# The first microseconds of a one-core transformer kernel: tokens in four transfers, squares shared out, narrowest bands scaled first

## The reference, cut to what matters

```python
def rms_norm(x, g):
    xf = x.astype(jnp.float32)
    y = xf * lax.rsqrt(jnp.mean(xf * xf, axis=-1, keepdims=True) + RMS_EPS)
    return (y * g.astype(jnp.float32)).astype(x.dtype)

def pool_mixer(h, w, scale):
    ...
    for g, win in enumerate(POOL_WINDOWS):      # (2, 4, 8, 16), 256 features each
        c = cs[:, :, g]                          # running sum over tokens
        lag = jnp.pad(c[:, :-win], ((0, 0), (win, 0), (0, 0)))
        mean = (c - lag) / jnp.minimum(n_avail, float(win))[:, None]
        outs.append(mean - hf[:, :, g])
    ...
    y = jnp.einsum('bsgc,gcd->bsgd', p, w).reshape(B, S, D)
    return y * scale
```

## Time and profile before

| what | value |
|---|---|
| median of 3 runs | 1299.62 us (1297.34, 1299.62, 1299.71) |
| the profiled execution, its own time | 1299.65 us |
| its span in the profile | 1297.9 us |
| PE busy (matmul) | 98% of the span |
| DVE busy | 71% |
| ACT busy | 47% |
| first matmul starts at | 6.14 us |

### The profile page before, as it was taken

One profiled execution on the slowest core, in us unless ns is written; L12 is line 12 of the kernel. 1 busy time (PEld: TensorE's weight loads), 2 busy tenths in 40 slices (PEclk: granted clock), 3 DMA queues, 4 the chain that ended last, 5 costly groups with the idle time before them and its releaser, 6 DMA issues.

```text
span 1297.9 us, 19342 instructions
## 1 busy us (share of the span) xinstructions
PE 1270.6 (98%) x7379; PEld 1109.1 (85%) x7379; DVE 916.4 (71%) x1217; ACT 605.3 (47%) x881; POOL 29.3 (2%) x29
## 2 busy tenths in 40 slices
PE   7999999999999999999999999999999999999997
PEld 7779999988888777788999998888888888888876
DVE  6897787874447766579788787454768388887554
ACT  6445454553334655444454455434323255666434
POOL 0510000000000000000000000000000000000000
PEclk9999999999999999999999999999999999999999
DMA  5322424332332111231332423223624221113311
GB/s 194 109 87 66 129 67 127 90 113 89 107 103 79 30 64 66 65 97 54 109 108 86 129 87 115 90 89 106 183 65 163 66 64 34 50 49 130 98 65 66
DMA packets 156963, 119.70 MB, mean 92 GB/s; under 512 B 15132, under 2 KB 153832, under 8 KB 156648
## 3 DMA queue, kind: packets, MB, share of 16 engines
q1 hardware_dynamic: 156848, 118.89, 29.9%
q10 hardware_dynamic: 56, 0.01, 0.0%
HBM read 114.70 MB, written 4.19 MB: 92 GB/s over the span
## 4 chain that ended last, share of the span: by engine, by line
PE 75%; DVE 13%; issue 4%; ACT 4%; DMA 2%; SPq 1%; DVEq 0%; ACTq 0%
PE psum L2338 22%; PE psum L2340 22%; PE psum L2339 22%; DMA w_raw<-in_ffn_w_up 2%; PE psum L2563 1%; PE psum L2586 1%; DVE w_lo L1596 1%; DVE w_lo L1409 1%; ACT w_hi L908 1%; PE psum L2748 1%; PE psum L2720 1%; ACT w_hi L802 1%; PE psum L2732 1%; DVE second_sum L1583 1%; DVE ffn_f L1551 1%
## 5 line engine op out<-in xcount | busy, mean ns | idle before, releaser
L2338 PE MATMUL psum<-terms_hi,w_hi 128*128 128x256 f32 x952 | 270.9, 285 | 3.0 <-DVE work L1607 2.6
L2339 PE MATMUL psum<-terms_lo,w_hi 128*128 128x256 f32 x952 | 270.1, 284 | 0.0
L2340 PE MATMUL psum<-terms_hi,w_lo 128*128 128x256 f32 x952 | 270.1, 284 | 0.0
L2338 PE MATMUL psum<-xg_hi,w_hi 128*128 128x512 f32 x544 | 220.8, 406 | 3.5 <-DVE squares L1536 1.9
L2340 PE MATMUL psum<-xg_hi,w_lo 128*128 128x512 f32 x544 | 212.3, 390 | 0.0
L2339 PE MATMUL psum<-xg_lo,w_hi 128*128 128x512 f32 x544 | 212.1, 390 | 0.0
L2338 PEld LDWEIGHTS psum<-terms_hi,w_hi 128*128 128x128 f32 x952 | 183.4, 193 | 4.5 <-DVE w_lo L1596 2.8
L2339 PEld LDWEIGHTS psum<-terms_lo,w_hi 128*128 128x128 f32 x952 | 183.4, 193 | 0.1
L2340 PEld LDWEIGHTS psum<-terms_hi,w_lo 128*128 128x128 f32 x952 | 183.4, 193 | 0.0
L2338 PE MATMUL psum<-act_hi,w_hi 128*128 128x512 f32 x352 | 137.2, 390 | 0.0
L2340 PE MATMUL psum<-act_hi,w_lo 128*128 128x512 f32 x352 | 136.9, 389 | 0.0
(11 more groups left out here) (404 smaller groups left out, 2201.2 us busy)
## 6 DMA issues: line engine op xcount, KB each, us to landing
w_raw<-in_ffn_w_gate SPq DMA_DIRECT2D x68, 256.0 KB, 3.4
w_raw<-in_ffn_w_up SPq DMA_DIRECT2D x68, 256.0 KB, 3.9
w_raw<-in_w_in SPq DMA_DIRECT2D x16, 1024.0 KB, 5.4
w_raw<-in_ffn_w_down SPq DMA_DIRECT2D x16, 768.0 KB, 4.5
w_raw<-in_ffn_w_down SPq DMA_DIRECT2D x16, 640.0 KB, 4.3
w_raw<-in_ffn_w_gate SPq DMA_DIRECT2D x5, 1024.0 KB, 5.1
w_raw<-in_ffn_w_up SPq DMA_DIRECT2D x5, 1024.0 KB, 5.2
w_raw<-in_mla_w_o SPq DMA_DIRECT2D x4, 1024.0 KB, 5.0
```

What stands on the lines that cost most here:

```text
L2338: pe.matmul(o, wh, xh, start=start, stop=False, skip_group_check=True)
L2339: pe.matmul(o, wh, xl, start=False, stop=False, skip_group_check=True)
L2340: return pe.matmul(o, wl, xh, start=False, stop=stop, skip_group_check=True)
```

## The change

Tokens come in four transfers of one block each, with a semaphore for each, and PE turns the seven chunks block by block. ACT squares blocks 0 and 2 and the first 512 features of block 3, DVE squares block 1 and the last 512 features of block 3, and DVE adds the two sums of block 3. Blocks 0 to 2 get their root and reciprocal ahead of block 3. The bands of the smallest width (144 columns, all that `pooled(0)` and `pooled(1)` use) are scaled ahead of the other three widths (432 columns). Two semaphores are folded into others (`ones_set` into `eps_set`, `mask_loaded` into `pos_loaded`).

```diff
-            for n in range(2):
-                sp.dma_start(x_tok[:, 2 * n:2 * n + 2, :], a["x"][0].rearrange("(i p) f -> p i f", p=P)[:, 2 * n:2 * n + 2]).then_inc(sem(f"x_loaded{n}"), 16)
-                if n == 0:
+            for i in range(NB):
+                sp.dma_start(x_tok[:, i, :], a["x"][0, i * P:(i + 1) * P, :]).then_inc(sem(f"x_loaded{i}"), 16)
+                if i == 0:
                     sp.dma_start(ident[:, :], a["c_ident"]).then_inc(sem("ident_loaded"), 16)
...
# ACT
-            act.wait_ge(sem("tok_squares"), NB)
-            act.activation(tok_stat[:, 1, :], tok_stat[:, 0, :], ACT.Sqrt, ...).then_inc(*mark("tok_root"))
+            act.wait_ge(sem("tok_squares"), 3)
+            act.activation(tok_stat[:, 1, 0:3], tok_stat[:, 0, 0:3], ACT.Sqrt, ...).then_inc(*mark("tok_root_early"))
+            act.wait_ge(sem("x_loaded3"), 16)
+            act.activation(h_tok[:, 3, 0:T], x_tok[:, 3, 0:T], ACT.Square, accum_out=tok_stat[:, 0, 3:4]).then_inc(*mark("tok_half"))
+            act.wait_ge(*at("tok_sum"))
+            act.activation(tok_stat[:, 1, 3:4], tok_stat[:, 0, 3:4], ACT.Sqrt, ...).then_inc(*mark("tok_root"))
+            act.wait_ge(*at("tok_rstd_early"))
+            act.wait_ge(sem("band_loaded"), 16)
+            odd_band(1, slice(0, 1))
             act.wait_ge(*at("tok_rstd"))
-            act.wait_ge(sem("band_loaded"), 16)
-            for i in (1, 3):
-                act.activation(band_tok[:, i, :, :], band[:, :, 0, :], ACT.Copy, scale=tok_stat[:, 2, i:i + 1])...
+            odd_band(3, slice(0, 1))
+            odd_band(1, slice(1, 4))
+            odd_band(3, slice(1, 4))
...
# PE
-            for n in range(2):
-                pe.wait_ge(sem(f"x_loaded{n}"), 16)
+            for i in range(NB):
+                pe.wait_ge(sem(f"x_loaded{i}"), 16)
                 for m in range(7):
-                    mm = turn_x(m, (2 * n, 2 * n + 1))
-                    if n:
+                    mm = turn_x(m, (i,))
+                    if i + 1 == NB:
                         mm.then_inc(sem("x_turned"), 1)
...
-                    pe.wait_ge(sem("band_odd" if i % 2 else "band_even"), i // 2 + 1)
+                    pe.wait_ge(sem("band_odd" if i % 2 else "band_even"), (0 if c < 2 else 2) + i // 2 + 1)
```

More of the change, by code:

```diff
@@ L746, in _ @@
         def _(pool):
-            pool.memset(ones[:, :], 1.0).then_inc(sem("ones_set"), 1)
+            pool.memset(ones[:, :], 1.0).then_inc(sem("eps_set"), 1)
             pool.memset(eps_col[:, 0:1], EPS).then_inc(sem("eps_set"), 1)
@@ L751, in _ @@
             pool.memset(eps_col[:, 3:4], 1.0).then_inc(sem("eps_set"), 1)
-            pool.wait_ge(sem("eps_set"), 4)
+            pool.wait_ge(sem("eps_set"), 5)
             pool.memset(eps_col[64:128, 3:4], -1.0).then_inc(sem("eps_set"), 1)
-            pool.wait_ge(sem("eps_set"), 5)
+            pool.wait_ge(sem("eps_set"), 6)
             MAGIC, TWO_PI = 1.5 * 2.0 ** 23, 6.283185307179586
@@ L758, in _ @@
             ang = sem("angle_step")
-            pool.wait_ge(sem("pos_loaded"), 32)
+            pool.wait_ge(sem("pos_loaded"), 48)
             pool.wait_ge(*at("mix_summed"))
@@ L814, in _, with odd_band @@
             for i in (0, 2):
-                act.wait_ge(sem(f"x_loaded{i // 2}"), 16)
+                act.wait_ge(sem(f"x_loaded{i}"), 16)
                 act.activation(h_tok[:, i, :], x_tok[:, i, :], ACT.Square, accum_out=tok_stat[:, 0, i:i + 1]).then_inc(sem("tok_squares"), 1)
-            act.wait_ge(sem("eps_set"), 5)
-            act.wait_ge(sem("tok_squares"), NB)
-            act.activation(tok_stat[:, 1, :], tok_stat[:, 0, :], ACT.Sqrt, scale=1.0 / D, bias=eps_col[:, 0:1]).then_inc(*mark("tok_root"))
+            act.wait_ge(sem("eps_set"), 6)
+            act.wait_ge(sem("tok_squares"), 3)
+            act.activation(tok_stat[:, 1, 0:3], tok_stat[:, 0, 0:3], ACT.Sqrt, scale=1.0 / D, bias=eps_col[:, 0:1]).then_inc(*mark("tok_root_early"))
+            act.wait_ge(sem("x_loaded3"), 16)
+            act.activation(h_tok[:, 3, 0:T], x_tok[:, 3, 0:T], ACT.Square, accum_out=tok_stat[:, 0, 3:4]).then_inc(*mark("tok_half"))
+            act.wait_ge(*at("tok_sum"))
+            act.activation(tok_stat[:, 1, 3:4], tok_stat[:, 0, 3:4], ACT.Sqrt, scale=1.0 / D, bias=eps_col[:, 0:1]).then_inc(*mark("tok_root"))
+            def odd_band(i, windows):
+                act.activation(band_tok[:, i, windows, :], band[:, windows, 0, :], ACT.Copy, scale=tok_stat[:, 2, i:i + 1]).then_inc(sem("band_odd"), 1)
+            act.wait_ge(*at("tok_rstd_early"))
+            act.wait_ge(sem("band_loaded"), 16)
+            odd_band(1, slice(0, 1))
             act.wait_ge(*at("tok_rstd"))
-            act.wait_ge(sem("band_loaded"), 16)
-            for i in (1, 3):
-                act.activation(band_tok[:, i, :, :], band[:, :, 0, :], ACT.Copy, scale=tok_stat[:, 2, i:i + 1]).then_inc(sem("band_odd"), 1)
+            odd_band(3, slice(0, 1))
+            odd_band(1, slice(1, 4))
+            odd_band(3, slice(1, 4))
             def late_copy(m):
@@ L1420, in chain @@
                 dve.tensor_tensor(sq_sum[:, :], sq_sum[:, :], squares[:, m % 2, :], ALU.add).then_inc(dv, 1)
[L1422 to L1425, removed]
+            dve.wait_ge(sem("x_loaded1"), 16)
+            dve.scalar_tensor_tensor(h_tok[:, 1, :], x_tok[:, 1, :], 1.0, x_tok[:, 1, :], ALU.mult, ALU.mult, accum_out=tok_stat[:, 0, 1:2])\
+               .then_inc(sem("tok_squares"), 1)
+            dve.wait_ge(sem("x_loaded3"), 16)
+            dve.scalar_tensor_tensor(h_tok[:, 3, T:2 * T], x_tok[:, 3, T:2 * T], 1.0, x_tok[:, 3, T:2 * T], ALU.mult, ALU.mult, accum_out=tok_stat[:, 0, 4:5])\
+               .then_inc(*mark("tok_low"))
+            dve.wait_ge(*at("tok_low"))
+            dve.wait_ge(*at("tok_half"))
+            dve.tensor_tensor(tok_stat[:, 0, 3:4], tok_stat[:, 0, 3:4], tok_stat[:, 0, 4:5], ALU.add).then_inc(*mark("tok_sum"))
+            dve.wait_ge(*at("tok_root_early"))
+            dve.reciprocal(tok_stat[:, 2, 0:3], tok_stat[:, 1, 0:3]).then_inc(*mark("tok_rstd_early"))
             def early_copy(m):
@@ L1429, in early_copy, with even_band @@
                 dve.tensor_copy(xT[:, m, :], bank[m][:, :]).then_inc(sem("xT_early"), 1)
+            def even_band(i, windows):
+                dve.tensor_scalar(band_tok[:, i, windows, :], band[:, windows, int(i == 0), :], tok_stat[:, 2, i:i + 1], None, ALU.mult).then_inc(sem("band_even"), 1)
             early_copy(0)
+            dve.wait_ge(*at("tok_rstd_early"))
+            dve.wait_ge(sem("band_loaded"), 16)
+            even_band(0, slice(0, 1))
+            even_band(2, slice(0, 1))
             dve.wait_ge(*at("tok_root"))
-            dve.reciprocal(tok_stat[:, 2, :], tok_stat[:, 1, :]).then_inc(*mark("tok_rstd"))
+            dve.reciprocal(tok_stat[:, 2, 3:4], tok_stat[:, 1, 3:4]).then_inc(*mark("tok_rstd"))
             early_copy(1)
[L1435 to L1438, removed]
+            even_band(0, slice(1, 4))
+            even_band(2, slice(1, 4))
             early_copy(2)
```

14 lines of the change are left out of this document (7 added, 7 removed).

## The result

The changed kernel takes 1301.53 us (median of 11 runs), the kernel before 1299.13 us (11 runs beside them). The ratio is 1.0021, with a 95% interval of 1.0012 to 1.0031: it is slower by 2.7 us, between 1.6 and 4.0. The forecast was 1299.5, that is 0.15 us faster, and no difference that can be told.

What follows compares the result with a forecast made beforehand. PE was taken as the bound, its matmuls filling 98% of the span. 0.19 us gained at `mixed(0)`, less 0.05 for a transfer, gave about 0.15: 1299.65 - 0.15 = 1299.5 us, range 1297.0 to 1300.4.

Steps and rivals of the forecast that it cites:

- Transfers: Token loads at the start: four blocks land at 4.57, 5.98, 7.23 and 8.48 us, an added transfer costing 0 to 0.16.
- Late tokens: Rival, token loads: at 0.3 us per transfer blocks 2 and 3 land late, slower by 0.3, 1299.9 us; chance 0.14.
- the head start: PE's bands start 0.9 us sooner; 0.19 left at `mixed(0)`, about 0.15 after an added transfer. Full 0.9 as rival: 0.12.
- DVE up to `cols`: DVE from block 3's addition at 9.48 us to the copy into `cols`, ending at 13.33, 0.14 us later than before.
- ACT up to `w_hi`: ACT's split band scaling: pieces of 0.30 and 0.55 us, everything behind 0.38 us later, `w_hi` at 15.32.
- PE: PE's bands start 0.9 us sooner, then PE waits for `cols` before chunk 7; `mixed(0)` at 16.72 us, 0.19 sooner.
- Behind that: After `mixed(0)`: ACT and DVE catch up, with 1.05 and 1.57 us to spare, and the rest follows PE.
- The rival of new gaps: Rival: PE's gaps between 9.5 and 13.4 us lower the clock, slower by 1.5, 1301.1 us; chance 0.06.
- the other rival: Rival: the low-clock stretch at 122 us goes away, faster by 1.5, 1298.1 us; chance 0.08.

Runs made afterwards that it cites:

- second profile: The changed kernel run once more, unaltered; last tokens at 9.47 us and `mixed(0)` at 18.20 us, one run without a ratio.
- the run with the bands alone: Kernel before, with each block's 144-column band scaled ahead of the other 432 columns, transfers and squares as before; ratio 1.0001 [0.9992, 1.0009].

## Why the prediction was wrong

- *Transfers.* This is the step that failed. "512 KB take 1.25 us, and the four blocks land at 4.57, 5.98, 7.23 and 8.48", with 0 to 0.16 us for an added transfer. The first was right (by 4.29). The rest came 1.99, 2.07 and 2.06 us late; in a second profile block 1 was on time and the last two came 0.99 late. A rate that I had read behind 1 MB on the queue was used where only 512 KB lay ahead. The bound for any added transfer I took from the identity's 0.32 us, less 0.16 for its bytes, though it too had 1 MB ahead of it. By the runs it is the place of the identity's short rows among short token transfers on one queue that costs: with the identity on ACT's queue the tokens landed at 8.85 and the time was that of before. What goes on inside the queue, and why the size swings from 1.0 to 2.1 us, stays open. `mixed(0)` after 17.2 was named as a sign of being wrong, and it came at 19.27.
- *"Late tokens", the rival.* Its direction was right, its price of 0.3 us was not. Its own figure was 1299.9, and the top of the range, 1300.4, follows from no sum of the prediction. With the tokens 2.06 us late and DVE's 0.52 of the next point, the head start of 0.15 becomes a loss of 2.06 + 0.52 - 0.15 = 2.43 us; `mixed(0)` was 2.36 late. On the median of 1299.13 before, 2.43 gives 1301.56, against 1301.53 measured. That this is so near is luck, since the tokens came only 0.99 late in the other profile. The rule on batching of the Trainium skill (DMA: Bandwidth & Descriptors, section "Bandwidth"), which I had set against the rows, pointed the right way. It isn't the mechanism: four transfers of 512 KB with the identity on ACT's queue landed in 7.82 us, two of 1 MB in 7.92.
- *DVE up to `cols`.* From the addition to the end of `cols` I had 3.85 us (9.48 to 13.33); measured 4.37 (11.56 to 15.93). The mis-sized term is the wide band, 0.34 forecast and 0.57 measured. The straight line assumed one speed. The Trainium skill (VectorE: DVE Perf Modes, section "Side-by-side: where the cycles go for N=2048 bf16") gives one-source operations two elements a cycle only with an outermost dimension that is even, or equal in source and destination. The runs agree: three widths took 0.57 us, two took 0.28, four 0.43. Source and destination both have three rows of 144 here, which would be equal; they differ only if the destination's rows, which lie end to end, count as one of 432. No run tests that.
- *ACT up to `w_hi`.* Pitches (start to start) of 0.30 and 0.55 were right: three pieces took 14.31 - 12.89 = 1.42 us, forecast 1.40.
- *PE.* Right in kind. The bands started sooner behind the last tokens than before (12.73 - 10.54 = 2.19 us, against 11.58 - 8.48 = 3.10), PE then stood before chunk 7 waiting for `cols`, 0.42 us here and 0.99 us in the second profile, and the head start was gone. From `cols` on, forecast 3.39 us to `mixed(0)`, measured 19.27 - 15.93 = 3.34.
- *Behind that.* The shift was carried: 2.36 at 19 us, 2.36 at 51 us, 2.51 at the last transposes. In the second profile 1.29 at `mixed(0)` became 2.31 there, so a microsecond can come from elsewhere.
- *The clock.* The rival of new gaps did not come true: from 10 to 20 us the granted clock was 1.00. The low stretch at 122 did go away, as the other rival had it, but a like one came at 82, so that nothing was gained:

```profile
82.50:85.50 3.00, 3.00 (x8) 2.33 (x8) 3.00 (x4) 2.14 (x3) 0.00 (x0) 0.50 0.90 259
```

In the kernel before this stretch ran at full clock, and it was the one at 122 that was low. The mean granted clock is 0.72 from 82 to 88 us in the changed kernel and 0.72 from 121 to 127 before, so the two cost about the same. In the run with the bands alone there was none at 122 either:

```profile
121.00:126.00 5.00, 4.93 (x41) 4.96 (x42) 5.00 (x6) 1.50 (x2) 0.00 (x0) 1.00 0.01 3
```

- *What can be told.* I took 0.2% for the least that a measurement shows. With 11 runs on each side the interval was 0.1% to either side, and 2.4 us came clear of zero. "Same" had 0.92 of my chances because no rival of mine reached 2.6 us. The largest unknown cost, that of the transfers, had been bounded by one row only.

## What to carry to other kernels

A transfer rate read in the middle of a full queue did not hold for short transfers at its head: with the first transfer cut in two and short rows behind it, its followers came 1 to 2 us late. Put short-row constants on another engine's queue, or keep the first transfer long (the latter was run only with the transfers by themselves). Measure landings alone and many times over, since one profile swings by a microsecond. When a VectorE operation is split along its outer dimension, look at whether an odd or an even number of rows is left, not only at the number of instructions.

## What was not expected of the hardware

- Four token transfers with a 64 KB transfer of 512-byte rows second left the DMA engines a quarter idle (DMA share 0.75, 227 GB/s) from 5 to 7 us in one profile, with all tokens issued by 3.1 us; in another of the same kernel the share was 1.00 at 361 GB/s, and the last tokens were late all the same. By themselves, the same four with that transfer on another queue landed in 7.82 us, against 9.70 (medians of 12).
- With the 64 KB transfer still second, but every other token transfer issued by ACT, they landed in 7.77 us (7.72 to 7.88), the narrowest spread of all forms.
- 432 columns in three rows of 144 took VectorE 0.57 us in `tensor_scalar`; 576 in four rows took 0.43, 288 in two 0.28.
- A gap of 2.95 us on PE was followed by a granted clock of 0.50 that cost another 3 us: 2.4 us of added work became 5.40 us, in one profile.
